# Whole-matrix ring units, a merged spatial product and eight fillers in a two-layer hybrid decoder trunk

## What is computed

```
h = layer_norm(x)
for l in range(2):
    p = h @ w_in[l]                       # 1024 -> 2560 columns
    A = attention(rotary(q), rotary(k), v)         # 512 columns, 8 heads
    B = gelu(u) * (causal(W_s) @ layer_norm(gelu(v)) + b)   # 256, 4 groups, chunks of 128
    C = silu(layer_norm(conv31(a * sigmoid(g))))   # 256 columns
    h = layer_norm(alpha * h + concat(A, B, C) @ w_out[l])
    # 16 experts, each token goes to 2 of them
    out = sum over experts e of gates[:, e] * ((silu(h @ w_gate[l, e]) * (h @ w_up[l, e])) @ w_down[l, e])
    h = layer_norm(alpha * h + out)
```

## Time and profile before

| | us |
|---|---|
| median of 3 runs | 721.97 |
| lowest and highest | 721.77, 723.27 |
| the profiled execution | 721.64 |
| its span, first to last instruction | 719.8 |
| TensorE matmuls busy | 670.3 (93%) |
| VectorE busy | 281.1 (39%) |
| ScalarE busy | 141.3 (20%) |
| bytes moved | 240.72 MB, mean 334 GB/s |

### The profile page before, as it was taken

How to read it: one execution, slowest core, us unless ns; L and a number is a source line. 1 busy time by engine, 2 the same in 40 slices (tenths; PEclk the granted TensorE clock), 3 DMA queues, 4 the chain that set the end, 5 groups by cost and what they waited for, 6 DMA issues and landing times.

```text
span 719.8 us, 7383 instructions
## 1 busy us (share of the span) xinstructions
PE 670.3 (93%) x3039; PEld 329.5 (46%) x3039; DVE 281.1 (39%) x585; ACT 141.3 (20%) x280; POOL 67.9 (9%) x65
## 2 busy tenths in 40 slices
PE   7999999999999999987689999989999999998882
PEld 4645587543333543332375446856333445332331
DVE  4496767410333022130627936771120330321226
ACT  3102453231110211110121026523201113100100
POOL 1603000410000000000050210006000000000001
PEclk9999999999999999999979999999999999999997
DMA  8999636099999999999999641433999999999991
GB/s 282 341 388 413 270 118 234 5 374 405 421 422 421 421 421 421 421 421 421 396 387 404 266 163 67 158 128 151 372 422 422 421 421 421 422 420 422 421 407 66
DMA packets 48572, 240.72 MB, mean 334 GB/s; under 512 B 4428, under 2 KB 8852, under 8 KB 23956
## 3 DMA queue, kind: packets, MB, share of 16 engines
q1 hardware_dynamic: 47956, 238.06, 82.4%
q10 hardware_dynamic: 576, 2.10, 0.7%
HBM read 239.10 MB, written 1.05 MB: 334 GB/s over the span
## 4 chain that ended last, share of the span: by engine, by line
PE 72%; DMA 18%; DVE 7%; issue 1%; ACT 1%; POOL 0%; DVEq 0%; POOLq 0%; ACTq 0%
PE bank L544 22%; PE bank L465 15%; PE bank L563 12%; DMA ring<-in_w_up 9%; DMA ring<-in_w_gate 8%; PE bank L479 5%; PE bank L522 5%; PE bank L625 4%; PE bank L583 3%; PE bank L552 1%; PE bank L443 1%; PE bank L697 1%; DVE stats L1217 1%; DVE h L1210 1%; PE bank L688 1%
## 5 line engine op out<-in xcount | busy, mean ns | idle before, releaser
L544 PE MATMUL bank<-ring,xe 128*64 128x512 f32 x1024 | 226.0, 594 | 14.9 <-DMA ring<-in_w_up 7.9
L544 PEld LDWEIGHTS bank<-ring,xe 128*64 128x64 f32 x1024 | 71.7, 137 | 162.4 <-issue 136.1
L563 PE MATMUL bank<-ring,area_b 128*64 128x512 f32 x512 | 113.4, 595 | 1.6 <-DVE area_b L1231 1.6
L465 PE MATMUL bank<-ring,xT_area 128*128 128x512 f32 x256 | 111.3, 593 | 0.0
L1225 DVE TENSOR_TENSOR area_b<-area_b,bank 128x512 f32<-128x512 f32 x16 | 11.0, 687 | 253.7 <-PE bank L544 253.7
L465 PEld LDWEIGHTS bank<-ring,xT_area 128*128 128x128 f32 x256 | 48.1, 190 | 57.4 <-issue 57.4
L563 PEld LDWEIGHTS bank<-ring,area_b 128*64 128x64 f32 x512 | 35.2, 137 | 68.4 <-issue 64.0
L950 POOL TENSOR_TENSOR rstd<-var_eps,half_neg 128x1 f32<-128x1 f32 x18 | 11.7, 660 | 544.9 <-DVE var_eps L1037 544.9
L1245 DVE SCALAR_TENSOR_TENSOR y_lo<-bank,slot_gate,y_hi 128x512 fp32r<-128x512 f32 x32 | 24.0, 751 | 89.2 <-ACT y_hi L871 89.2
L1293 DVE SCALAR_TENSOR_TENSOR mix<-glu,tapsT,mix 128x256 f32<-128x256 f32 x120 | 47.7, 471 | 0.0
L871 ACT ACTIVATE y_hi<-bank,slot_gate 128x512 fp32r<-128x512 f32 x32 | 22.0, 687 | 98.1 <-PE bank L563 98.1
(11 more groups left out here) (159 smaller groups left out, 577.2 us busy)
## 6 DMA issues: line engine op xcount, KB each, us to landing
ring<-in_w_gate SPq DMA_DIRECT2D x32, 2048.0 KB, 22.8
ring<-in_w_up SPq DMA_DIRECT2D x32, 2048.0 KB, 23.8
ring<-in_w_down SPq DMA_DIRECT2D x32, 2048.0 KB, 24.5
ring<-in_w_in SPq DMA_DIRECT2D x9, 2048.0 KB, 20.4
ring<-in_w_out SPq DMA_DIRECT2D x4, 2048.0 KB, 21.0
ring<-in_w_in SPq DMA_DIRECT2D x2, 1024.0 KB, 7.1
h<-in_x SPq DMA_DIRECT2D x2, 512.0 KB, 4.1
ln_par<-in_ln_mix_g ACTq DMA_DIRECT2D x2, 512.0 KB, 7.5
```

The lines of the kernel that those rows point to most:

```text
L465: mm = pe.matmul(dst[:, :], xT[:, c, b * P:(b + 1) * P], w[:, c, :], start=c == 0, stop=c == KC - 1)
L544: mm = pe.matmul(bank[2 + u % 2][e * SLOTS:(e + 1) * SLOTS, :], xe[:, k, at + e * SLOTS:at + (e + 1) * SLOTS], w[:, e, c, :], start=k == 0 ...
L563: mm = pe.matmul(bank[5 + n][e * SLOTS:(e + 1) * SLOTS, :], hidT[:, k, e * SLOTS:(e + 1) * SLOTS], w[:, e, c, n * BANK:(n + 1) * BANK], st ...
```

## The change

Three edits.

1. In pairs 1 to 6 of each layer (`WHOLE`) a unit is one expert's whole matrix: gate of the first expert, gate of the second, up, up, down, down. Pairs 0 and 7 keep the halves. In each partition a unit is then one piece of 16 KB. `gate_up` takes both experts' gate units, sums all eight chunks, releases both units, and then does the same for up; `down` takes both down units, computes the first 512 output columns, raises `down_half`, computes the other 512 and releases both. In pair 4 the second gather comes after the first half of gate. ScalarE waits for the second release of a pair instead of the third.
2. The spatial product waits for both blocks and issues four matmuls of 2 x 64 columns instead of eight of 64.
3. Eight fillers into bank 5 stand ahead of layer 1's first transposes.

```
+WHOLE = (1, 2, 3, 4, 5, 6)
-KEEP_START, KEEP_MIX, KEEP_ROUTER, KEEP_SLOTS = 18, 6, 18, 6
+KEEP_START, KEEP_NORM, KEEP_MIX, KEEP_ROUTER, KEEP_SLOTS = 18, 8, 6, 18, 6
@@ load_pairs (SP)
                         sp.wait_ge(ps.used, turn + (ps.used0 + k - RING + 1))
+                        at = (ps.unit0 + k) % RING
+                        if ps.main and j in WHOLE:
+
+                            w = (w_gate, w_up, w_down)[u // 2][l, first + u % 2].rearrange("(p c) n -> p (c n)", p=P)
+                            sp.dma_start(ring[:, at, :], w).then_inc(ps.landed[at], 16)
+                            continue
@@ gate_up (TensorE)
+                    if ps.main and j in WHOLE:
+                        for m in range(2):
+                            w = [landed_unit(PAIR_UNITS * j + 2 * m + e) for e in range(2)]
+                            for k in range(KC):
+                                if j % GROUP == 0 and m == 0:
+                                    if k == 4:
+                                        gather(g, range(4, KC))
+                                    nth_group("xe", g, k + 1, KC)
+                                for e in range(2):
+                                    mm = pe.matmul(bank[2 + m][e * SLOTS:(e + 1) * SLOTS, :],
+                                                   xe[:, k, at + e * SLOTS:at + (e + 1) * SLOTS],
+                                                   w[e][:, k * DE:(k + 1) * DE], start=k == 0, stop=k == KC - 1)
+                                    if k == KC - 1:
+                                        mm.then_inc(ps.used, 1)
+                        return
@@ down (TensorE)
+                    if ps.main and j in WHOLE:
+                        w = [landed_unit(PAIR_UNITS * j + 4 + e) for e in range(2)]
+                        for n in range(2):
+                            for k in range(FC):
+                                for e in range(2):
+                                    mm = pe.matmul(bank[5 + n][e * SLOTS:(e + 1) * SLOTS, :],
+                                                   hidT[:, k, e * SLOTS:(e + 1) * SLOTS],
+                                                   w[e][:, k * D + n * BANK:k * D + (n + 1) * BANK],
+                                                   start=k == 0, stop=k == FC - 1)
+                                    if n and k == FC - 1:
+                                        mm.then_inc(ps.used, 1)
+                            if n == 0:
+                                mm.then_inc(s["down_half"], 1)
+                        return
@@ start of a layer (TensorE)
+                if l:
+                    keep_clock(5, KEEP_NORM)
@@ spatial product (TensorE)
-                for b in range(TB):
-                    pe.wait_ge(sgv_ready, TB * l + b + 1)
-                    for g in range(GROUPS):
-                        mm = pe.matmul(bank[4][:, b * SG + g * HD:b * SG + (g + 1) * HD], sgwT[:, l, g, :],
-                                       uv[:, b, SG + g * HD:SG + (g + 1) * HD], start=True, stop=True)
+                pe.wait_ge(sgv_ready, TB * (l + 1))
+                mixed = bank[4][:, :].rearrange("p (b n) -> p b n", b=TB)
+                for g in range(GROUPS):
+                    mm = pe.matmul(mixed[:, :, g * HD:(g + 1) * HD], sgwT[:, l, g, :],
+                                   uv[:, :, SG + g * HD:SG + (g + 1) * HD], start=True, stop=True)
@@ experts (ScalarE)
-                    act.wait_ge(ps.used, units_before + (ps.used0 + PAIR_UNITS * j + 3))
+                    act.wait_ge(ps.used, units_before + (ps.used0 + PAIR_UNITS * j + (2 if ps.main and j in WHOLE else 3)))
```

More of the change, by code:

```diff
@@ L376, in load_pairs @@
                         src = w[:, bass.ds(first, 2), half * 2048:(half + 1) * 2048]
-                        at = (ps.unit0 + k) % RING
                         sp.dma_start(ring[:, at, :].rearrange("p (e n) -> p e n", e=2), src)\
```

## The result

The changed kernel takes **717.31 us** in the median of five runs (716.16 to 719.73), against 721.97 us (720.44 to 723.27) for five runs of the kernel before. The ratio is 0.9939, with a 95% interval of [0.9914, 0.9964]: 4.7 us faster, where 6.4 were forecast. The profiled execution is the slowest of the five, 719.73 us, with a span of 717.9.

A forecast was written before the change was run, and what follows sets the result against it. The DMA's rate was taken to end the expert phases, TensorE and what feeds it the rest. 721.64 - 4.4 - 2.0 - 0 = 715.2 us, on the three-run median 715.6; range 711.8 to 722.2.

The forecast's parts named there:

- Part 1 (a): Expert phase: 16 KB pieces raise the DMA rate from 421 to 427 GB/s, 2.2 us less a layer.
- Rival A: Expert phase: piece size changes nothing, the rate stays at 421 GB/s; 720.0 us, chance 0.20.
- half-way case: Expert phase: a third to a half of the rate's gain, say 0.9 us a layer; 718.2 us, chance 0.06.
- units 12 to 41 stream back to back: Ring loads in each expert phase: 30 units gain 0.074 us each, 2.2 us a layer.
- (b): Ring, pair 1: releases come two at a time and later, yet no bubble at unit 14, 1.8 us to spare.
- Part 1 (c): Pairs 6 and 7: TensorE's idle time only lumps, waits up to 2.9 us; the tail is unchanged.
- Rival C: Pair 6's lumped waits let TensorE's clock fall: 721.0 us, or 725.2 with the rate unchanged; chance 0.10.
- Part 2: Spatial product in both layers: four matmuls of 128 columns for eight of 64, 1.0 us saved a layer, -2.0 us.
- Part 3: Layer boundary: eight fillers shorten the idle to 3.8 us, the clock still falls; taken as 0, ends -2.75 and +1.5.
- rival B: Layer boundary: the fillers hold the clock across it, 2.75 us less; 712.8 us, chance 0.12.
- Part 1: Expert phases: whole matrices in pairs 1 to 6, -2.2 us a layer, -4.4 together.

## Why the prediction was right, and which steps failed

The forecast was 715.6, the time is 717.31, inside the range of 711.8 to 722.2 and faster, as forecast. With the experiments the sum can be made again: expert stretches 2 x -1.24 = -2.5, spatial product 2 x -0.84 = -1.7, together -4.2 (the kernel without fillers measured -5.0 by the medians, -4.7 by the ratio), and the fillers +0.3 by the ratios of that pair of kernels, +2.0 by the pair with pair 1 in halves. The forecast's terms were -4.4, -2.0 and 0.

**Part 1 (a), the rate: right.** The line through two rates gave 427 GB/s, and both layers read 427; with 8 KB pieces and the same grouping it is 421. (The slope on record, 36.9 ns, is for each further 1000 bytes; for a KB of 1024 bytes, as the piece sizes are given, it is 37.8. The 613.5 ns and the 427 follow from either.) Rival A and its half-way case are out.

**Part 1 (a), "units 12 to 41 stream back to back", with (b), "no bubble": the step that was mis-sized.** The term was -2.2 a layer and measured -1.24. With pair 1 in halves it is -2.22. The working looked for one tight spot, unit 14's late release, and found 1.8 us to spare. The runs show the 1.0 us tied to pair 1's being whole, and 0.7 of it or so there also with 8 KB pieces, so that the order of release and not the piece is the likelier carrier. The failed step is the margin: I had counted it by landings, and a landing is the last engine's. The queue runs dry with the first engine, which is done with unit 13 1.8 us sooner in the changed kernel (36.9 for 38.7), as much as I had to spare. The bubble at unit 14 is there, 0.2 us in the mean engine; 0.2 more are lost by unit 13, while the DMA share is still 0.93 to 0.96 (1.01 in the plateau). The remaining 0.6 is the last engine's lag, a term that the working didn't have, and why it is longer with pair 1 whole stays open.

**Part 1 (c), the lumped waits: right** in place, and in layer 0 in size: 1.50 and 2.72 us for 1.5 and 2.9, last wait at 335.22 for 335.1. In the other kernels with pairs 1 to 6 whole the first of the two is 1.57 to 2.46 us, so the agreement to a tenth is in part luck. Of the two waits forecast in pair 7 one is gone, because of the clock, as follows.

**Rival C, the clock falls in them: it happens, and costs nothing that can be seen.** Up ran at the 1.2 GHz level for 3.4 us and took 8.46 us, 1.4 more. In the kernel with pair 1 in halves, where it held (7.09 us), pair 7 waits 0.71 + 1.31 us; in the changed kernel 0.76. The wait for the ring takes up what the clock costs. The rival's own condition, more than 3.5 us of work lost, wasn't reached: its 10.3 us at half clock were carried over from the boundary, while every fall inside an expert phase in these traces lasted 3.4 us. The forecast called itself wrong if the clock reads 0.5 in pairs 5 to 7; that was too strong a test, since what decides is whether a wait is left behind it.

**Part 2: right**, 0.84 us for 1.0. The near row was the 128-column transposes, 0.11 us a record; it is 0.136.

**Part 3: a right-looking zero from a wrong mechanism.** "Fillers fill 1.75 of the 5.5 idle us and end long before 361" failed. They started at 358.02, 5.62 us behind the last combine, and the transposes began at 361.40. I had put the gap down to the norm alone, since it does end then; the branch over the second loop holds TensorE 0.6 us longer, because the code behind it has to be fetched (the instruction packet above). The row to distrust was that of the gap itself: an engine that waits for nothing the profile shows has "issue" beside it, and a releaser that comes 0.6 us before hides behind it. Being late, the fillers also ran at the 1.2 GHz level, 0.42 us each and not 0.22. So they cost up to 3.4 us, of which the clock can give some back: in the changed kernel it was at the 2.4 GHz level again from 363.1 to 366.5, in the one without fillers only from 369.9. Over the profiled executions the boundary is 24.8 to 27.9 us, mean 26.3, in the seven kernels that have the branch and no fillers at all, and 29.4 and 27.7 in the two with eight behind the branch: +2.2. The forecast of 3.8 us of idle, which was to drop the clock all the same, was never met by the changed kernel, whose gap was 5.6; the kernel with the fillers ahead of the branch has 3.96 us, and there the clock fell (rival B is out).

**The missing 1.7 us.** Part 1 fell short by 1.9 and part 2 by 0.3; the fillers cost between 0.3 and 2.2. That is at least 2.5 where 1.7 are missing, so some 0.8 us came from elsewhere: the kernel without fillers shows as much beyond its sum (-5.0 for -4.2). Its interval, -6.4 to -3.1 us, holds both, so this difference needs no cause.

## What to carry over

Before work is put into an idle stretch, find out what keeps the engine idle and where in its order the new work stands: a second holder that ends just behind the first (here a branch over a loop that isn't entered, 0.6 us behind the norm) turns free fillers into 3.4 us of path. Larger transfers gain where the stream is steady; at its start and in its last pair small units are worth more, so coarsen from the middle and read each end by itself. Count the room in a queue by the engine that finishes first, and the end of a transfer by the one that finishes last. A clock that fell in a wait for a transfer was no loss here, where a later wait for the same stream took it up.

## What the runs showed of the hardware

- Transfers into the ring run at 387 GB/s with 2 KB pieces, 421 with 8 KB and 427 with 16 KB: the line drawn through the first two gave the third.
- Skipping a loop that isn't entered holds TensorE for up to 5.62 us (5.56 to 5.62 in the kernels with fillers behind it), and it doesn't all pass beside the matmuls ahead of it: with 22 fillers ahead the gap ended 1.5 us later, 2.29 us behind the last of them. The Trainium skill, page "Runtime: NRT & Kernel Launch", says under its warning that branching breaks sequential prefetch that a taken branch out of the current window stalls until its target is fetched. The traces agree: a 16 KB instruction packet starts 2.9 to 3.1 us behind the last combine in the kernels with the branch (4.47 with 22 fillers ahead) and is absent in the two without.
- A unit lands with the slowest of 16 DMA engines, 1.2 to 2.7 us behind their mean at unit 45.
- The clock fell in or behind waits of 2.7 us in some executions (up 8.46 us in the changed kernel) and not in others (7.09 with pair 1 in halves and, in layer 0, with 22 fillers); with 22 fillers, in layer 1, it fell behind one of 2.04 us.
- In four of the fourteen traces it also fell for 3.4 us in layer 0's first slab (12.6 to 16.8 us), behind waits of no more than 1.7 us, as in the kernel with 22 fillers, whose slab took 15.74 us for 14.05. Layer 0's first expert matmul then starts at 139.4 to 140.0, and at 138.0 to 138.3 in the others that have part 2. The forecast had concluded from one trace that a gap of 2.0 us there keeps the clock.
- At the boundary the stretch at the 1.2 GHz level is 6.8 to 13.7 us long in the kernels without fillers, whose gaps are all between 5.0 and 5.6 us. Much of the scatter of the runs, some 1.5 us to either side, may come from this, which was not measured run by run.
- Layer 1's first slab took 14.05 us at the full clock and up to 17.11 (the kernel without fillers) when it came back late, so that one look at a boundary can't price a change of 1 us there.
